# A two-block transformer on one core: shared up product in units 1 and 2, two slab rooms outside the ring, late constants, head sums spread over gate tiles

## The chip, the cores and the metric

One Trainium2 chip; the program runs on one core. The metric is device time in microseconds of the whole program (one launch), the median of three runs. Engines: TensorE (PE) multiplies, VectorE (DVE), ScalarE (ACT) and GpSimd (POOL) work on vectors, and SyncE (SP) issues most of the weight transfers.

## The reference, cut to what matters

Sequence of T = 256 tokens, width D = 1024, batch 1, everything in float32.

```python
# block 1
h = rms_norm(x, g1) * (1 + scale1) + shift1              # six modulation vectors = silu(c) @ w_ada + b
na_q, na_k, na_v, q_lat, kv_lat, k_rot, gate_na, gate_mla = split(h @ w_in)
y_na  = neighbourhood_attention(8 heads of 64)
qm, km = latent attention: 8 heads of 96, each head's row RMS-normed over its 96 values
x += gate1 * ((sigmoid(gate_na) * (y_na @ w_proj_na) + sigmoid(gate_mla) * (y_mla @ w_proj_mla)) @ w_out)
h2 = rms_norm(x, g2) * (1 + scale2) + shift2
# 64 experts, 8 per token (4 of 8 groups first), each 1024 -> 256 -> 1024
routed = sum over chosen experts of gate * (silu(h2 @ w_eg) * (h2 @ w_eu)) @ w_ed
shared = (silu(h2 @ w_sg) * (h2 @ w_su)) @ w_sd
x += gate2 * (routed + shared)
# block 2, for x and for a context ctx of 256 rows (the context does not depend on x)
layer 0: gMLP gating beside Fourier mixing, on x and on ctx
layer 1: windowed attention of x over x and ctx, 16 heads
out = rms_norm(x, final_g)
```

## The kernel before, in words

Each engine's program is written out by hand, one `block` function per engine, with semaphores between them. There is no planner at run time; the order of each engine's instructions is the order in the code.

**Weights as slabs.** All large weights are cut into slabs of 1 MiB (128 partitions x 2048 floats). They go through a ring of 11 slots (`ring`, `RING = 11`). PE's code asks for slabs in its own order (`ask`, `take_slab`) and says by `ends` which of its steps gives a slot back. SP's function (L1388) loads the slabs in the order asked, each once the slot's former slab has ended (`load`, `given_back`). From the first expert on, slots are handed out in the order in which they are given back, not round the ring. One slab has a room of its own: `first_slab` in the arena.

**Block 1.** PE computes the projections from `hT` (the normed input, features on partitions), slab by slab. `gate_tiles(s)`, s = 0 to 7, makes the 16 sigmoid gates, two tiles of 8 products each per slab (each float32 product stands as two records in the trace). Between slabs 4 and 5 stand the head sums of the latent attention: for each of four groups of two heads, the sums of squares of the queries (8 records of one column, L831) and of the keys (one product of 512 columns, L838). ACT squares a group into `sqt` (queries in half 0, keys in half 1), PE sums it, and ACT may write the half again once it is read. ACT takes roots, and DVE reciprocals (L2088). Then come both attentions (`early_attention`), the projections (L857), `w_out` (L873), and the router (`router`, L883).

**Routing.** From the router's result DVE makes scores, group choice, top 8, and the order of experts by how many tokens each has (`ordered`). Slots of tokens per expert, and the gates (`gates_made`), follow. PE has as filler four modulation slabs (`LAST_FILL`), then the shared gate product (`shared("shg", ...)`) and the shared up product (`shared("shu", ...)`, both L922), before it turns the gates by expert and gathers token rows for the first units (`gather`, L982).

**Expert stage.** 24 units; a unit of kind P holds two experts, X two of unequal slots, Q four with 32 slots each. Unit 0 takes the two experts fixed in advance (their slabs are loaded before the ranking is known: six slabs, `first_ones`); all other experts' addresses wait for `ordered`. Per unit: first half of the gate and up product (one slab per expert, L1140), the gate column, second half (one slab each), gathers for a later unit, `scatter` of the unit before into four banks (L1004), turns, and the down product (one slab each, L1183). After each half stand the steps of the table `CONTEXT`: the row `2: z0 z1 fa0 | fb0 fa1` puts z0, z1 and fa0 after the first half of unit 2 and fb0 and fa1 after its second half. They are block 2's layer 0 for the context: z and v tiles (16 and 4, one slab per two tiles, L1095 and L1101), Fourier steps fa and fb, sp, o tiles (L1039), the sum of squares and norm, and `shd`, the shared down product. DVE and ACT follow in `context_out`.

**Constants.** POOL loads `cs2` (Fourier tables, rotary tables, window mask, spatial bias; 1408 KB, L1511) and `spat` after the residual of block 1. ACT loads the router weights after the fourth pair of the early attention.

After the experts come the context keys (L1258), layer 0 and layer 1 of block 2 for x, and the output.

Of the kernel before, what the change touches and what calls it, by code (L numbers as in the profile page):

```python
# [19 lines left out]
ALU = mybir.AluOpType  # L20
# [74 lines left out]
15: | o1 o2  # L95
16: o3 |
18: o4 | o5
19: o6 |
20: | o7
21: squares0 | sum0  # L100
# [36 lines left out]
C2_AT, C2_W = offsets(C2_WIDTHS)  # L137
V_AT, V_W = offsets(V_WIDTHS)
# [3 lines left out]
def build(nc, x_d, ctx_d, consts_d, consts2_d, vecs_d, pos_d, rpb_d, spat_d, router_d, slabs_d, exp_d, out_d):  # L142
    with ExitStack() as ctx:
# [39 lines left out]
        def cc(name, a=0, b=None):  # L183
            src, at = (cs, C_AT) if name in C_AT else (cs2, C2_AT)
            lo, hi = at[name]
            return src[:, lo + a:(hi if b is None else lo + b)]
# [101 lines left out]
        rows = ar(4096, KT * (T + 1), KT, T + 1)  # L288
# [8 lines left out]
        cs2 = ar(11008, C2_W + 512)  # L297
        spat_bias = cs2[:, C2_W:C2_W + 512]
        spat = ar(11008 + C2_W + 512, 512, 4, 128)
# [8 lines left out]
        with nc.sbuf_tensor("bias_room", [P, 8 * RUN + 1024], F32) as bias_room:  # L308
            braw = bias_room[:, 0:8 * RUN].rearrange("p (a b) -> p a b", a=8)
            bmask = bias_room[:, 8 * RUN:8 * RUN + 1024].rearrange("p (a b) -> p a b", a=2)  # L310
            wr = bias_room[:, 0:512].rearrange("p (a b) -> p a b", a=8)
# [133 lines left out]
        def _(pe):  # L445
# [379 lines left out]
            o = open_group("mq_sums", 3)  # L825
            for g in range(4):
                pe.wait_ge(S("sq_m"), 2 * g + 1)
                for h in range(2):
                    for t in range(TT):
                        c = 4 * g + 2 * h + t  # L830
                        mm = mmul(o[:, c:c + 1], sqt[0:96, 0, 256 * h + P * t:256 * h + P * t + P], ones[0:96, 0:1],  # L831
                                  start=True, stop=True)
# [4 lines left out]
                pe.wait_ge(S("sq_m"), 2 * g + 2)  # L837
                close_group(mmul(open_group(("msum", 4 + g), 1 + g % 2)[0:96, :], ones[0:96, 0:96], sqt[0:96, 1, :], start=True, stop=True), ("msum", 4 + g))  # L838
            for s in (5, 6, 7):
                gate_tiles(s)  # L840
# [44 lines left out]
            for k in range(KT - 1):  # L885
                router(k)
# [6 lines left out]
            close_group(router(KT - 1), "rtT")  # L893
# [115 lines left out]
            def expert_slabs(m, j):  # L1009
                if m == 0:  # L1010
                    if j == 0:
                        first_ones.extend(ask(("exp", r, i)) for i in range(3) for r in UNITS[0][1])
                        held["ahead"] = ask(("ab", 4))
                    got = [(arrived(n), n) for n in first_ones[2 * j:2 * j + 2]]
                else:
                    got = [take_slab(("exp", r, j)) for r in UNITS[m][1]]
                return [w.rearrange("p (k c) -> p k c", c=512) for w, _ in got], [n for _, n in got]
# [48 lines left out]
            def context_step(m, kind, i, b):  # L1066
# [10 lines left out]
                if kind in ("squares", "norm"):  # L1077
                    return
                if kind == "o":
# [3 lines left out]
                if kind == "z":  # L1083
                    if i == 0:
                        pe.wait_ge(S("first_in"), 16)
                    elif i == 4:
                        held[kind] = held["ahead"]
                        arrived(held[kind])
                    elif i % 2 == 0:
                        held[kind] = take_slab(("ab", 2 + i // 2))[1]  # L1090
                    w = first_slab if i < 2 else eight(held[kind])
# [11 lines left out]
                elif kind == "fa":  # L1103
                    if i == 0:
                        pe.wait_ge(S("const2_in"), 32)
# [10 lines left out]
                if kind in ("z", "v") and i % 2 and (kind, i) != ("z", 1):  # L1116
# [272 lines left out]
        def _(sp):  # L1389
            expert_of = {}  # L1390
# [16 lines left out]
            def load(n):  # L1407
# [1327 lines left out]
```

## Time and profile before

| | us |
|---|---|
| median of 3 runs | 1102.38 (1100.65 to 1103.85) |
| the profiled execution, own time | 1107.04 |
| its span | 1105.2 |
| PE busy | 1057.4 (96%) |
| DVE busy | 394.6 (36%) |
| ACT busy | 283.6 (26%) |
| mean DMA rate over the span | 303 GB/s (335.12 MB) |
| mean granted clock | 0.988 |

The span runs from the first to the last instruction. Busy time of PE counts pipelined matmuls whose ends are modelled, so a slow clock shows as busy, not idle. The DMA share is the mean busy share of the 16 DMA engines, and it can come out slightly above 1. A line number such as L1140 is that of the program of before.

### The profile page before, as it was taken

How to read it: one execution, taken by the hardware profiler on the slowest of the kernel's cores; microseconds unless marked ns; L12 is line 12 of the kernel's file. 1: busy time of each engine (PE TensorE's matmuls, PEld its weight loads, DVE VectorE, ACT ScalarE, POOL GpSimd, SP SyncE). 2: the span in 40 equal slices, each digit the busy share in tenths (PEclk: the TensorE clock that was granted, in tenths of full speed). 3: DMA queues.
4: the chain of work that ended last, by engine and by line, in shares of the span. 5: the costliest groups of instructions: out<-in, count | busy, mean ns of one | idle time of the engine just before them, and what ended most of it. 6: DMA issues, size and time to landing. Idle time of an engine off the chain costs nothing.

```text
span 1105.2 us, 15950 instructions
## 1 busy us (share of the span) xinstructions
PE 1057.4 (96%) x6296; PEld 730.0 (66%) x6296; DVE 394.6 (36%) x1034; ACT 283.6 (26%) x656; POOL 52.4 (5%) x85
## 2 busy tenths in 40 slices
PE   6999999999999999899989999999789999999998
PEld 4786776688755665465546565555358888887567
DVE  1398966523532223112212212121333021523941
ACT  3124134510431112112211111123222111213941
POOL 0000202013100000000000000001000001100001
PEclk9999989999999999999999999999999999999999
DMA  9999387964769999999999999999996334310000
GB/s 385 354 420 420 125 338 273 419 271 153 297 256 411 419 421 420 421 420 421 421 421 421 421 421 421 421 421 421 419 417 272 125 118 152 112 39 1 1 2 38
DMA packets 48555, 335.12 MB, mean 303 GB/s; under 512 B 5440, under 2 KB 6816, under 8 KB 8672
## 3 DMA queue, kind: packets, MB, share of 16 engines
q1 hardware_dynamic: 46080, 329.01, 73.2%
q10 hardware_dynamic: 2176, 3.37, 1.0%
q0 software_dynamic: 224, 1.70, 0.4%
q8 instruction: 51, 0.84, 0.3%
q14 instruction: 24, 0.20, 0.0%
HBM read 333.02 MB, written 1.05 MB: 302 GB/s over the span
## 4 chain that ended last, share of the span: by engine, by line
PE 81%; DMA 12%; DVE 4%; ACT 1%; issue 1%; SPq 1%; DVEq 0%; ACTq 0%
PE bank L1140 12%; PE bank L567 12%; DMA ring<-experts 11%; PE bank L1183 6%; PE bank L1282 5%; PE bank L1095 4%; PE bank L982 3%; PE bank L486 3%; PE bank L1370 3%; PE bank L857 3%; PE bank L1325 2%; PE bank L873 2%; PE bank L1004 2%; PE bank L697 2%; PE bank L633 2%; PE bank L1039 2%
## 5 line engine op out<-in xcount | busy, mean ns | idle before, releaser
L1140 PE MATMUL bank<-ring,arena 128*32 128x512 f32 (+1 forms) x1120 | 177.2, 608 | 17.4 <-DMA ring<-experts 16.4
L1140 PEld LDWEIGHTS bank<-ring,arena 128*32 128x32 f32 (+1 forms) x1120 | 54.0, 122 | 121.5 <-issue 120.4
L567 PE MATMUL bank<-hT,ring 128*128 128x256 f32 x576 | 128.4, 383 | 0.7 <-ACT hT L1564 0.7
L567 PEld LDWEIGHTS bank<-hT,ring 128*128 128x128 f32 x576 | 109.6, 192 | 21.5 <-issue 6.9
L1183 PE MATMUL bank<-ring,conds 128*32 128x512 f32 (+1 forms) x560 | 87.5, 595 | 4.3 <-DMA ring<-experts 2.6
L1725 ACT ACTIVATE arena<-bank,mod 128x256 f32<-128x256 f32 x96 | 40.2, 470 | 98.6 <-PE bank L982 98.5
L2384 DVE SCALAR_TENSOR_TENSOR conds<-bank,gcol,conds 128x256 f32<-128x256 f32 x24 | 11.6, 484 | 143.7 <-ACT conds L1756 125.8
L2399 DVE TENSOR_TENSOR yhalf<-bank,yhalf 128x512 fp32r<-128x512 f32 x48 | 33.2, 692 | 78.8 <-ACT yhalf L1764 78.8
L1501 POOL TENSOR_TENSOR hT<-hT 128x256 f32<-128x256 f32 x30 | 21.7, 723 | 822.1 <-ACT hT L1558 820.6
L982 PE MATMUL bank<-picked,halves 128*128 128x256 f32 x384 | 57.8, 293 | 0.7 <-ACT arena L1725 0.7
L1183 PEld LDWEIGHTS bank<-ring,conds 128*32 128x32 f32 (+1 forms) x560 | 27.4, 119 | 46.7 <-issue 39.2
L1282 PE MATMUL bank<-hT,ring 128*128 128x256 f32 x256 | 57.0, 379 | 0.0
L982 PEld LDWEIGHTS bank<-picked,halves 128*128 128x128 f32 x384 | 48.8, 188 | 10.7 <-issue 8.9
L2158 DVE SCALAR_TENSOR_TENSOR resid<-bank,mod,resid 128x256 f32<-128x256 f32 (+1 forms) x48 | 19.7, 437 | 93.6 <-PE bank L1370 25.8
L1282 PEld LDWEIGHTS bank<-hT,ring 128*128 128x128 f32 x256 | 48.3, 190 | 6.6 <-issue 0.2
L1095 PE MATMUL bank<-hT,ring 128*128 128x256 f32 x224 | 50.3, 382 | 0.1
L1004 PE MATMUL bank<-yhalf,selT 128*128 128x512 f32 x192 | 48.5, 394 | 0.0
L1095 PEld LDWEIGHTS bank<-hT,ring 128*128 128x128 f32 x224 | 42.1, 190 | 7.9 <-issue 2.1
L1756 ACT ACTIVATE conds<-bank 128x256 f32<-128x256 f32 x24 | 9.2, 383 | 145.3 <-PE bank L1140 145.3
L1764 ACT CAST yhalf<-bank 128x512 fp32r<-128x512 f32 x48 | 28.1, 585 | 59.1 <-PE bank L1183 59.1
L1984 DVE SCALAR_TENSOR_TENSOR arena<-ring,conds,arena 128x256 f32<-128x256 f32 x84 | 40.7, 485 | 3.0
L1004 PEld LDWEIGHTS bank<-yhalf,selT 128*128 128x128 f32 x192 | 34.4, 188 | 7.8 <-issue 1.6
(415 smaller groups left out, 1444.5 us busy)
## 6 DMA issues: line engine op xcount, KB each, us to landing
ring<-experts SPq DMA_DIRECT2D x188, 1024.0 KB, 14.5
ring<-stream SPq DMA_DIRECT2D x119, 1024.0 KB, 12.3
ring<-experts SPq DMA_DIRECT2D x8, 512.0 KB, 15.4
arena<-consts POOLq DMA_DIRECT2D x1, 1408.0 KB, 9.4
resid<-x SPq DMA_DIRECT2D x1, 1024.0 KB, 5.1
resid<-ctx ACTq DMA_DIRECT2D x1, 1024.0 KB, 9.9
arena<-stream SPq DMA_DIRECT2D x1, 1024.0 KB, 8.3
bias_room<-rpb ACTq DMA_DIRECT2D x2, 438.0 KB, 5.6
```

The source lines that it names most:

```text
L486: mm = mmul(o[32 * g:32 * g + 32, 0:256], (silc if which == "ada1" else silc2)[:, 4 * kk + g, at:at + 32], w[:, 4 * kk + g, :], start=firs ...
L567: mm = mmul(o[:, 0:n_tok], w[:, k, t * P:(t + 1) * P], hT[:, k, 0:n_tok], start=(k == 0), stop=(k == KT - 1))
L857: mm = mmul(o[:, 0:256], w[:, 512 * k + P * t:512 * k + P * t + P], yT[:, y0 + k, :], start=(k == 0), stop=(k == 3))
L982: mm = mmul(o[:, 256 * (d % 2):256 * (d % 2) + n], halves[:, q, t, P * d:P * d + P], picked[:, t, 0:n], start=(t == 0 and q == 0), stop=(t ...
L1004: mm = mmul(bank[b][:, :], selT[:, b // 2, :], yhalf[:, q, 512 * (b % 2):512 * (b % 2) + 512], start=m == 0 and q == 0, stop=last and q == 1)
L1095: mm = mmul(o[:, 0:T], w[:, k, P * (i % 2):P * (i % 2) + P], hT[:, k, T:2 * T], start=(k == 0), stop=(k == KT - 1))
L1140: mm = mmul(o[at:at + n_slots, :], xg_of(m, kk)[:, at:at + n_slots], w[g][:, k, :], start=(kk == 0), stop=(kk == KT - 1))
L1183: mm = mmul(o[at:at + n_slots, :], aT[:, f, at:at + n_slots], w[g][:, 2 * c + f, :], start=(f == 0), stop=(f == 1))
L1282: mm = mmul(o[:, 0:T], eight(n)[:, k, (i % 2) * P:(i % 2 + 1) * P], hT[:, k, 0:T], start=(k == 0), stop=(k == KT - 1))
L1725: last = a.activation(to[:, i, 0:n], bk(("xg", j, c))[:, 256 * i:256 * i + n], ACT.Identity, bias=mod1[:, 24 + 2 * c + i:25 + 2 * c + i])
L1984: last = v.scalar_tensor_tensor(out=at, in0=w[:, k, :], scalar=silc[:, k, 15:16], in1=at, op0=ALU.mult, op1=ALU.add)
L2399: last = v.tensor_tensor(yhalf[:, 1, 512 * c:512 * c + 512], bk(("y", m, c))[:, :], yhalf[:, 0, 512 * c:512 * c + 512].bitcast(F32), ALU.s ...
```

## The change

The table of context steps, with the shared up product (`shu`) in it and everything later moved:

```diff
-CONTEXT = """1: z4 z5 |
-2: z0 z1 fa0 | fb0 fa1
-3: fb1 z2 |
-4: z3 z6 z7 | fa2
-5: | fb2
-6: fa3 | fb3 v0
-8: v1 | v2 v3
-9: shd0 z8 | z9 z12
-11: z13 |
-12: sp0 sp1 z10 z11 z14 |
-13: | z15 sp2
-14: | sp3 fold0 o0
-15: | o1 o2
-16: o3 |
-18: o4 | o5
-19: o6 |
-20: | o7
-21: squares0 | sum0
+CONTEXT = """1: shu0 |
+2: | shu1 z4 z5
+3: z0 z1 | fa0
+4: fb0 | fa1
+5: fb1 z2 |
+6: | z3 z6 z7 fa2
+7: | fb2 fa3
+8: fb3 v0 | v1
+9: v2 | v3
+10: shd0 |
+12: z8 z9 | z12 z13 sp0 sp1
+13: | z10
+14: z11 z14 |
+15: z15 | sp2
+16: sp3 | fold0 o0
+17: o1 |
+18: o2 o3 | o4
+19: o5 o6 |
+20: o7 squares0 |
+21: sum0 |
 22: norm0 | norm1"""
```

PE no longer computes the up product before the gathers; its slab is asked for behind five slabs of unit 0 and kept until the second half of unit 2:

```diff
             shared("shg", 0, 0, range(6, KT))
-            shared("shg", 1, 7, range(0, 2))
             sort_by_rank("slots_by_rank", "slots_by_expert", 0, 5)
-            shared("shg", 1, 7, range(2, KT))
+            shared("shg", 1, 7, range(0, KT))
             ends(ng, ("shg", 1))
-            _, shared_slab["shu"] = take_slab(("shu", 0))
-            shared("shu", 1, 1, range(KT))
-            shared("shu", 0, 3, range(KT))
-            ends(shared_slab["shu"], ("shu", 0))
```

DVE's part of it (`by_token`, `shared_hidden`) moves to the same two context steps. Two slabs get rooms outside the ring: the first expert slab of unit 0 goes to `keys_room` (the later keys and values), the slab of z4 and z5 to the first half of `hT`:

```diff
+            idle_slab = hT[:, :, 0:T]
...
-                        first_ones.extend(ask(("exp", r, i)) for i in range(3) for r in UNITS[0][1])
-                        held["ahead"] = ask(("ab", 4))
-                    got = [(arrived(n), n) for n in first_ones[2 * j:2 * j + 2]]
+                        first_ones.extend(ask(("exp", r, i)) for i in range(3) for r in UNITS[0][1][i == 0:])
+                        held["shu"] = ask(("shu", 0))
+                        pe.wait_ge(S("early_in"), 16)
+                        got = [(keys_room[:, :], None), (arrived(first_ones[0]), first_ones[0])]
+                    else:
+                        got = [(arrived(n), n) for n in first_ones[2 * j - 1:2 * j + 1]]
...
                     if not expert_of:
+                        full(sp, "sum2")
+                        sp.dma_start(idle_slab, slabs_d[slabs_at["ab"] + 4].rearrange("p (k c) -> p k c", k=8)).then_inc(S("idle_in"), 16)
                         sp.wait_ge(S("ordered"), 1)
...
+                if old is not None and slab_end[old] == ("pm", 7) and not early:
+                    early.append(n)
+                    done(sp, ("na", "s", 7))
+                    sp.dma_start(keys_room[:, :], exp_d[expert(UNITS[0][1][0]), 0]).then_inc(S("early_in"), 16)
```

The constants are split; rotary tables and mask (`cs_late`, 1536 columns of 128 x 4 bytes, 0.79 MB) come after the experts. The places of `cs2`, `spat_bias`, `spat`, `rows` and `wr` in the arena change to fit:

```diff
-            pool.dma_start(cs2, consts2_d).then_inc(S("const2_in"), 16)
+            pool.dma_start(cs2, consts2_d[:, 0:DFT_W]).then_inc(S("const2_in"), 16)
+            pool.dma_start(spat_bias, consts2_d[:, C2_W:C2_W + 512]).then_inc(S("const2_in"), 16)
             pool.dma_start(spat, spat_d).then_inc(S("const2_in"), 16)
             partial_sums("sq4c", side=1)
+            pool.wait_ge(S("sq3"), 1)
+            pool.dma_start(cs_late, consts2_d[:, DFT_W:C2_W]).then_inc(S("late_in"), 16)
```

The head sums are split into groups and placed among the gate tiles of slabs 5 and 6 (`key_sums(g)` one product of 512 columns, `query_sums(g)` the 8 records of one column, `gate_part` half a tile: 4 of its 8 products):

```diff
+            key_sums(0)
+            key_sums(1)
+            gate_slab[5] = take_slab(("in", 13))[1]
+            gate_part(5, 0, 1, range(0, 4))
+            key_sums(2)
+            key_sums(3)
+            gate_part(5, 0, 1, range(4, KT))
+            gate_part(5, 1, 2, range(0, 4))
+            query_sums(0)
+            gate_part(5, 1, 2, range(4, KT))
...
+            query_sums(1)
+            gate_slab[6] = take_slab(("in", 14))[1]
+            gate_part(6, 0, 0, range(0, 4))
+            query_sums(2)
+            gate_part(6, 0, 0, range(4, KT))
+            gate_part(6, 1, 7, range(0, 4))
+            query_sums(3)
+            gate_part(6, 1, 7, range(4, KT))
...
+            gate_tiles(7)
```

ACT squares keys 0 and 1, then takes gate slab 4, keys 2 and 3, queries 0 and 1, the root of the key sums, gate slab 5, queries 2 and 3, gate slab 6, the root of the query sums, gate slab 7. DVE's work on the query sums moves behind its four reciprocals.

The router's eighth product moves ahead of the row sums, and the transfer of its weights from the fourth to the seventh pair of the attention:

```diff
-            for k in range(KT - 1):
-                router(k)
+            for k in range(KT):
+                mm = router(k)
+            close_group(mm, "rtT")
             pe.wait_ge(S("sq2_part"), KT - 2)
...
-            close_group(router(KT - 1), "rtT")
```

## Rows read from the trace of the kernel before

**Rows 1.** Page, part 1: busy us (share of the span) and instructions of each engine.

```profile
PE 1057.4 (96%) x6296; PEld 730.0 (66%) x6296; DVE 394.6 (36%) x1034; ACT 283.6 (26%) x656; POOL 52.4 (5%) x85
```

**Rows 2.** Windows: length, busy of five engines, then clock, DMA share, GB/s.

```profile
293.00:299.00 6.00, 6.00 (x44) 4.82 (x37) 4.79 (x23) 5.56 (x10) 0.00 (x0) 1.00 0.89 367
...
314.00:321.00 7.00, 6.07 (x38) 2.91 (x38) 3.86 (x13) 3.67 (x7) 0.00 (x0) 1.00 0.11 44
...
345.00:430.00 85.00, 85.00 (x598) 49.85 (x596) 24.01 (x83) 16.14 (x37) 0.00 (x0) 1.00 1.01 420
430.00:795.00 365.00, 349.47 (x2114) 198.78 (x2110) 79.54 (x185) 73.20 (x159) 4.34 (x6) 1.00 1.01 421
...
843.00:850.00 7.00, 7.00 (x34) 6.15 (x34) 3.23 (x9) 1.04 (x4) 0.00 (x0) 1.00 0.49 180
```

**Rows 3.** Waits of PE, 345 to 830: us in total, times, longest.

```profile
PE bank L1140 <- DMA ring<-experts: 16.4, 11, 5.2
PE bank L1183 <- DMA ring<-experts: 2.6, 3, 1.7
```

**Rows 4.** Chain that ended last, 780 to 835: start us, us, what.

```profile
795.42 16.00 DMA ring<-experts
```

**Rows 5.** Windows, as in rows 2, of the head sums.

```profile
143.00:146.00 3.00, 3.00 (x13) 2.00 (x12) 0.76 (x2) 1.33 (x3) 0.00 (x0) 0.58 0.96 360
...
150.00:154.00 4.00, 4.00 (x9) 2.50 (x8) 1.39 (x6) 2.01 (x3) 0.00 (x0) 0.54 1.01 428
```

**Rows 6.** Chain that ended last, 136 to 180, as in rows 4.

```profile
140.62 0.79 PE bank L831 x8
141.40 0.94 PE bank L838 x2
142.34 0.89 PE bank L831 x8
...
144.85 1.50 PE bank L831 x8
...
151.57 8.02 PE bank L567 x32
159.59 0.56 PE bank L511 x4
160.15 7.10 PE bank L567 x32
...
174.91 1.00 PE bank L486 x16
```

**Rows 7.** Timeline of ACT: start us, us, engine, line, operation, out<-in.

```profile
141.50 0.63 ACT L1639 ACTIVATE arena<-arena 96x512 f32<-96x512 f32 x1 [0.46 <-PE bank L831]
```

**Rows 8.** Timeline of DVE, as in rows 7.

```profile
154.52 3.35 DVE L2088 RECIPROCAL pT<-pT 96x512 f32<-96x512 f32 x1 [1.41 <-ACT pT L1553]
```

**Rows 9.** Timeline of PE, from the shared products to unit 0's down product.

```profile
300.65 9.83 PE L922 MATMUL bank<-arena,ring 128*128 128x257 f32 x44
...
316.42 3.65 PE L1140 MATMUL bank<-ring,arena 128*64 128x512 f32 x16 [0.93 <-ACT arena L1725]
...
326.79 3.65 PE L1183 MATMUL bank<-ring,conds 128*64 128x512 f32 x16
```

**Rows 10.** Timeline of DVE: the gates are divided.

```profile
303.93 0.42 DVE L2279 TENSOR_SCALAR pr<-pr,pT 128x64 f32<-128x64 f32 x2
```

**Rows 11.** Timeline of SyncE: issues of expert slabs around unit 0.

```profile
299.29 11.71 SPq L1426 DMA_DIRECT2D ring<-experts  x4
...
310.66 0.34 SPq L1426 DMA_DIRECT2D ring<-experts  x1
...
320.25 0.85 SPq L1426 DMA_DIRECT2D ring<-experts  x2
```

**Rows 12.** Page, part 6: KB each, us from issue to landing.

```profile
arena<-consts POOLq DMA_DIRECT2D x1, 1408.0 KB, 9.4
```

**Rows 13.** Timeline of PE: three context tiles in a row, unit 4.

```profile
400.52 10.63 PE L1095 MATMUL bank<-hT,ring 128*128 128x256 f32 x48
```

More of the change, by code:

```diff
@@ L137 @@
 C2_AT, C2_W = offsets(C2_WIDTHS)
+DFT_W = C2_AT["cos2"][0]
 V_AT, V_W = offsets(V_WIDTHS)
@@ L824, in _, with key_sums, query_sums @@
                 gate_tiles(s)
-            o = open_group("mq_sums", 3)
-            for g in range(4):
-                pe.wait_ge(S("sq_m"), 2 * g + 1)
+            def key_sums(g):
+                pe.wait_ge(S("sq_m"), g + 1)
+                o = open_group(("msum", 4 + g), 4 + g % 2)
+                close_group(mmul(o[0:96, :], ones[0:96, 0:96], sqt[0:96, g % 2, :], start=True, stop=True), ("msum", 4 + g))
+            def query_sums(g):
+                pe.wait_ge(S("sq_m"), 5 + g)
+                o = open_group("mq_sums", 3) if g == 0 else bk("mq_sums")
                 for h in range(2):
@@ L836, in _, with gate_part @@
                     close_group(mm, "mq_sums")
[L837 to L840, printed above, removed]
+            def gate_part(s, t, b, ks):
+                n = gate_slab[s]
+                o = open_group((f"gt{s}", t), b) if ks[0] == 0 else bk((f"gt{s}", t))
+                for k in ks:
+                    mm = mmul(o[:, 0:256], eight(n)[:, k, t * P:(t + 1) * P], hT[:, k, 0:256], start=(k == 0), stop=(k == KT - 1))
+                if ks[-1] == KT - 1:
+                    close_group(mm, (f"gt{s}", t))
+            gate_slab = {}
+            key_sums(0)
[8 more added lines that the diff above has]
+            gate_part(5, 1, 2, range(4, KT))
+            ends(gate_slab[5], ("gt5", 1))
+            for i in SIDE_SUMS[5]:
+                side_sum(i)
+            query_sums(1)
[6 more added lines that the diff above has]
+            gate_part(6, 1, 7, range(4, KT))
+            ends(gate_slab[6], ("gt6", 1))
+            for i in SIDE_SUMS[6]:
+                side_sum(i)
+            gate_tiles(7)
             pe.wait_ge(S("qk_ready"), 8)
@@ L1078, in context_step @@
                     return
+                if kind == "shu":
+                    if i == 0:
+                        shared_slab["shu"] = held["shu"]
+                        arrived(held["shu"])
+                    shared("shu", i, b, range(KT))
+                    if i == 1:
+                        ends(shared_slab["shu"], ("shu", 1))
+                    return
                 if kind == "o":
@@ L1115, in context_step @@
                 close_group(mm, (kind + "c", i))
-                if kind in ("z", "v") and i % 2 and (kind, i) != ("z", 1):
+                if kind in ("z", "v") and i % 2 and (kind, i) not in (("z", 1), ("z", 5)):
                     ends(held[kind], (kind + "c", i))
@@ L1628, in _, with squares_of @@
                 gate_tiles(s)
-            for gg in range(4):
-                for kind, src in ((0, qm), (1, km)):
-                    if gg == 1 and kind == 0:
-                        gate_tiles(4)
-                    act.wait_ge(S("m_in"), 4 * kind + gg + 1)
-                    if gg and kind == 0:
-                        act.wait_ge(S("mq_read"), gg)
-                    elif gg:
-                        full(act, ("msum", 3 + gg))
-                    a.activation(sqt[0:96, kind, :], src[0:96, 2 * gg:2 * gg + 2, :].rearrange("p a b -> p (a b)"), ACT.Square).then_inc(S("sq_m"), 1)
+            def squares_of(src, gg):
+                v = src[0:96, 2 * gg:2 * gg + 2, :].rearrange("p a b -> p (a b)")
+                a.activation(sqt[0:96, gg % 2, :], v, ACT.Square).then_inc(S("sq_m"), 1)
+            for gg in (0, 1):
+                act.wait_ge(S("m_in"), 4 + gg + 1)
+                squares_of(km, gg)
+            gate_tiles(4)
+            for gg in (2, 3):
+                act.wait_ge(S("m_in"), 4 + gg + 1)
+                full(act, ("msum", 2 + gg))
+                squares_of(km, gg)
+            for gg in (0, 1):
+                full(act, ("msum", 6 + gg))
+                squares_of(qm, gg)
+            root(1, pT[:, :, :].rearrange("p a b -> p (a b)"), "mk", 2048, 96)
+            gate_tiles(5)
+            for gg in (2, 3):
+                act.wait_ge(S("mq_read"), gg - 1)
+                squares_of(qm, gg)
+            gate_tiles(6)
             full(act, "mq_sums")
@@ L2323, in fold_tokens, with shared_hidden @@
                 v.tensor_tensor(to[:, P + 1:2 * P], src[:, 1:P], back, ALU.subtract).then_inc(S(tag), 1)
+            def shared_hidden():
+                dve.wait_ge(S("shg_made"), 2)
+                for t in range(2):
+                    done(dve, ("shu", t))
+                    v.scalar_tensor_tensor(out=shu[:, t, :], in0=shu[:, t, :], scalar=shifted[:, 2 + t:3 + t], in1=shg[:, t, :],
+                                           op0=ALU.add, op1=ALU.mult).then_inc(S("sh_act"), 1)
             def context_out(kind, i):
```

62 lines of the change are left out of this document (31 added, 31 removed).

## The prediction

> **What bounds the kernel now.** I read the page first: TensorE (PE) is busy 96% of 1105.2 us [rows 1], so there is little idle time to win by itself; what matters is where PE's work is slow and where the end is set by something else. The table of stretches shows DMA engines that are full from 345 to 795 us, 421 GB/s at a share of 1.01 [rows 2]: the expert stage streams weights without a break. The waits of PE say the same from the other side: 16.4 us for expert slabs in the gate and up products, and the chain that ended last runs over a 16.00 us piece of expert DMA right up to 811.42, where the last down product starts [rows 3, 4]. So the stage ends when its stream ends. At 421 GB/s a slab of 1 MiB (1.0486 MB) takes 2.49 us, and PE's pace in the stage costs nothing as long as it gives slots back in time. The end moves only if the stream starts earlier, has fewer bytes, or has fewer holes. Ahead of about 299 us nothing on the path waits for DMA; there the chain is PE, instruction by instruction. In it one stretch is odd: the head sums at 143 to 154 us run at a granted clock of 0.58 to 0.54 [rows 5].
>
> **Head sums spread over gate tiles.** The chain of that stretch [rows 6]: a query group (8 matmuls of one column) takes 0.79 us at full clock and 1.50 at half, a key group (2 of 512) 0.94; the gate tiles behind them take 8.02 instead of 7.10. From 140.62 to the first scores at 175.91 PE needs 35.3 us. The work afterwards is the same: four key groups, 4 x 0.94 = 3.8; four query groups, 4 x 0.84 = 3.4 (mean of the 0.79 and 0.89 at full clock); three gate slabs, 3 x 7.10 = 21.3; two side sums, 2 x 0.56 = 1.1; the mod1 slab 1.0. Sum 30.5, that is 4.8 less, if the clock stays full. Are the new waits covered? The squares of keys 0 and 1 need no sums and stand ahead of gate slab 4 on ACT; keys 2 and 3 and queries 0 and 1 each wait for one group of sums and have at least half a gate tile (1.78 us) against a 0.63 us square [rows 7]. Queries 2 and 3 stand behind the square root, a change of tables and gate slab 5 on ACT; that lies beside 7.1 us of gate slab 5 on PE. VectorE's four reciprocals of 3.35 us [rows 8] follow the root, which comes some 4 us sooner, and have the gate tiles beside them; its rq operations, now behind them, have some 3 us. I take -4.8. Bounds: 0 (the clock falls anyway) to -5.0. PE then runs 4.8 us ahead to the router; the slabs there are not late, since PE has no DMA wait in it.
>
> The Trainium skill ("TensorE: Matmul & The Clock Gate", the section on a second HAM failure mode, psum-queue depth-cycling) says that an engine that idles briefly between groups of matmuls, again and again, can make the clock swing between its two levels. PE shows no idle time in 140 to 154 us and the clock falls all the same, so the trace neither proves nor excludes it; by that rule eight hand-overs among gate tiles could bring the fall back, which is my first rival.
>
> **Router order.** The eighth router product now stands ahead of the row sums, which close about 0.5 us later; the row scale and what follows on VectorE (rtS copy, scores, mask, order) come 0.4 us later. PE has filler there, so I charge 0.4 to the routing chain (bounds 0 and 0.6). The router weights are fetched some 15 us later, still 60 us ahead of use: 0.
>
> **Shared up product out of the prelude.** The 44 records from 300.65 hold 12 of the gate product and 32 of the up product: at 0.22 us each the up product is 7.1 us [rows 9]. Taken out, PE reaches the turn of the gates at 303.3; but VectorE finishes the gates only at 304.35 [rows 10], 1.1 us later, and with the 0.4 above at 304.75. So gathers and unit 0 come 7.1 - 1.5 = 5.6 us sooner: from 316.42 to 310.8 in the old time (all times here leave out the 4.8, which moves everything alike). The two halves come back as 3.55 us each in units 1 and 2, where the stream sets the end: 0, as long as slots are free in time.
>
> **Slab rooms and slots, which set the stream.** Expert loads of unit 1 need the ranking, at 299.29. SyncE then issues four slabs only, from 299.29 to 310.66, the last two on slots that the shared products give back, and nothing until unit 0's first half returns slots at 320.25 [rows 11]. Four slabs are 10.0 us of transfer in 20.96: 11.0 us dry; the window 314 to 321 at a share of 0.11 shows it [rows 2]. Another 0.3 is lost before unit 0's down product ends. Afterwards: one expert slab lies in the room of the later keys and one context slab in hT, so with the up slab kept in the ring four slots are free at the ranking instead of two, and the gate slab's slot makes five (free at 303.3). The bytes still to come are the same on both sides (186 expert slabs and 13 others), so only the holes count. From 299.7: five slabs last to 312.15, the first slot of unit 0 comes back at 310.8 + 3.65 = 314.45: 2.3 dry. One slab, to 316.95, then two slots at 318.0: 1.1 dry. Two slabs, to 323.0, then two slots at 310.8 + 14.0 = 324.8 (unit 0 took 316.42 to 330.4): 1.8 dry. Behind them unit 1 gives four slots 3.6 us later, and two slabs cover 5.0. Dry time 5.2, and 0.4 for the later ranking: 5.6 against 11.3. Gain 5.7. Bounds: 0, if the freed time is lost again to a full ring, to -9, if unit 0 started at once and all but the first hole closed.
>
> Can PE use it? It starts 5.6 sooner, has 7.1 more to do, and has 19 us of DMA waits in the stage [rows 3]; it would still wait about 12 us, so the stream remains the bound.
>
> **Late constants.** Of 1408 KB [rows 12] 0.79 MB (1.9 us) move behind the experts. Where they were, the stretch 293 to 299 is not full, at a share of 0.89 [rows 2], so all that was asked for was over before the ranking's loads: 0 on the path. Where they go, DMA drops to a share of 0.49 at 843 to 850 [rows 2] and PE waits for no slab after the experts: 0. Without that cover it would cost 1.9.
>
> **Sum.** -4.8 - 5.7 = -10.5 us. The profiled execution took 1107.04 us with a span of 1105.2; it would take 1096.5. It is 4.7 us above the median of the timed runs, 1102.38, at which the same sum gives **1091.9 us**.
>
> **Rivals.** (1) The clock falls in the spread sums too. For: a query group is one column wide and the clock fell in the midst of such groups [rows 5, 6]. Against: each now has 1.8 us of dense gate work on both sides, and the gate tiles behind ran at their full-clock 7.10 again. The first term is lost: 1102.4 - 5.7 = 1096.7. (2) The ring is full more often than I count, and the stream's gain goes: 1102.4 - 4.8 = 1097.6. For: steps moved behind second halves put off the release of slots. Against: DMA stayed at 1.01 over 345 to 430, with a run of 10.63 us of context tiles in it [rows 2, 13]. (3) Slower: the same mechanism at its worst, in units 2 and 6. In unit 2, after the second half, stand 10.65 us of tiles, then 4.6 of gathers, scatter and turns and 3.6 of down product: 18.9 us in which three slots (7.5 us) come back, so 11.4 dry if no other is free; in unit 6 19.9 us against six slots (14.9), 5.0 dry. Together 16.4: 1091.9 + 16.4 = 1108.3. It decides from 13.8 us dry on; the same row of 10.63 us speaks against it, and the ring starts with two slots more.
>
> **How the numbers follow.** Forecast 0.64, rival 1 0.17, rival 2 0.11, both at once (about no change) 0.04, rival 3 0.04. A measurement here tells 0.3% (3.3 us) from no change. Faster by more: the first three, less a little for a partial loss of both: 0.89; within it 0.07; slower 0.04. The range, 1088.5 to 1098.5, holds the forecast with its bounds and rivals 1 and 2; below, it takes in that more of the holes closes.
>
> **What would show it.** Right: granted clock 1.00 from 140 to 171, the first scores near 171; the ranking's first load near 295 with four slabs in a row; unit 0 at 306; no window under a share of 0.9 after 325; the last expert wait over near 801, and PE waiting about 12 us for experts. Wrong: half-clock rows in the gate tiles (rival 1); a share under 1.0 in units 2 to 7 (rivals 2, 3); or PE without any wait for experts at the end, which would say that PE has become the bound.

## The result, and the profile after

The changed kernel took 1099.6 us (median of 20 runs; one execution of 2777.72 us stands alone and is left out of what follows, the others lie between 1093.77 and 1102.18). The kernel before took 1103.66 us beside it (median of 20, 1100.2 to 1108.65). The ratio is 0.9948, interval [0.9931, 0.9965]: 5.7 us faster, where 10.5 were forecast, and the time is above the upper end of the range by 1.1 us. The two medians by themselves lie 4.1 us apart. Here and below, a gain in us that stands beside a ratio is the ratio's unless medians are named; the two can differ by a microsecond or more, as the runs of one kernel spread over 2 to 9 us. The profiled execution took 1099.61 us, its span is 1097.8, 7.4 less than that of before. The first row of the page, busy time by engine, answers to [rows 1]:

```profile
PE 1055.3 (96%) x6296; PEld 726.0 (66%) x6296; DVE 394.4 (36%) x1034; ACT 286.6 (26%) x658; POOL 54.0 (5%) x87
```

PE is 2.1 us less busy with the same 6296 matmuls. The windows (length; busy of PE, PEld, DVE, ACT, POOL; clock; DMA share; GB/s) answer to [rows 2, 5]:

```profile
143.00:146.00 3.00, 3.00 (x12) 1.98 (x11) 0.93 (x3) 0.87 (x3) 0.00 (x0) 1.00 0.93 380
176.00:178.00 2.00, 2.00 (x16) 0.73 (x17) 1.80 (x10) 1.22 (x5) 1.50 (x3) 0.51 0.73 307
286.00:288.00 2.00, 2.00 (x10) 1.80 (x9) 1.35 (x12) 1.31 (x3) 0.00 (x0) 0.50 1.00 414
314.00:321.00 7.00, 6.56 (x38) 3.44 (x36) 1.57 (x4) 2.06 (x5) 0.00 (x0) 1.00 0.90 327
345.00:430.00 85.00, 84.41 (x606) 49.53 (x606) 22.93 (x76) 15.59 (x35) 0.00 (x0) 1.00 1.01 420
430.00:795.00 365.00, 352.56 (x2104) 201.69 (x2100) 76.51 (x180) 71.73 (x156) 4.34 (x6) 0.99 1.01 420
803.00:806.00 3.00, 1.74 (x12) 0.52 (x16) 0.00 (x0) 0.00 (x0) 0.00 (x0) 0.68 1.04 427
```

Two of the forecast's steps are in the first and the fourth row: the head sums now run at a clock of 1.00, and the hole at 314 to 321 us is closed (share 0.90, from 0.11). What was not forecast is in the second, third and last: the clock is down to half at 176 us, where attention starts, at 286 us, in the routing, and again at the last expert wait. The chain that ended last, from the head sums to the first scores and the first slabs behind them (start us, us, what), answers to [rows 6]; L855 is the gate tiles, L836 the key sums, L844 the query sums, L574 a gate slab by itself, L610 the scores, L493 slabs of modulation:

```profile
134.49 7.10 PE bank L574 x32
141.59 1.72 PE bank L836 x4
143.31 1.73 PE bank L855 x8
...
150.22 0.79 PE bank L844 x8
151.00 1.83 PE bank L855 x8
...
163.74 7.10 PE bank L574 x32
170.84 1.00 PE bank L493 x16
171.84 1.07 PE bank L610 x7
...
175.23 0.10 DVE mod L1983
175.33 0.04 issue
175.38 1.47 PE bank L610 x6
176.85 4.88 PE bank L493 x64
```

A query group takes 0.79 us, a gate half tile 1.8, the gate slab 7.10: all at full clock. Then PE waits for the modulation vector that DVE ends at 175.33, and the 64 matmuls behind it take 4.88 us; at full clock they take 3.66 (a row below). At the end of the stream the same view, of after and then of before, shows the last down product:

```profile
792.08 11.94 DMA ring<-experts
804.02 0.24 issue
804.26 5.22 PE bank L1232 x32
```

```profile
811.42 0.24 issue
811.66 3.64 PE bank L1183 x32
```

The last wait ends 7.4 us sooner, and 1.6 of that are given back in one product. PE's waits of 345 to 830 us (total, times, longest), which answer to [rows 3], fall from 19.0 to 14.1 us, near the 12 forecast:

```profile
PE bank L1189 <- DMA ring<-experts: 10.7, 4, 5.2
PE bank L1232 <- DMA ring<-experts: 3.4, 1, 3.4
```

SyncE issues five slabs in a row behind the ranking (four from 298.49 to 302.19, the fifth at 302.88), as predicted, where four were spread over 11 us before [rows 11]. Then it still waits for a slot, until unit 0's first half gives some back at 312.71:

```profile
298.49 3.70 SPq L1477 DMA_DIRECT2D ring<-experts  x4
312.71 4.37 SPq L1477 DMA_DIRECT2D ring<-experts  x3
```

So smaller holes are left, as the forecast had them: the DMA share is 0.78 at 313 to 316 us and 0.57 at 322 to 325.

Where the 7.4 us of span come from, stretch by stretch, each from PE's timelines of the two profiles:

| stretch | before, us | after, us | difference |
|---|---|---|---|
| start to the end of gate slab 4 | 140.45 | 141.43 | +1.0 |
| to the first scores | 35.4 | 30.3 | -5.1 |
| first scores to the second score group | 8.2 | 9.9 | +1.7 |
| second group to the router's start | 98.56 | 98.56 | 0 |
| router to the shared products | 10.7 | 12.3 | +1.5 |
| shared products to unit 0 | 23.1 | 16.4 | -6.7 |
| unit 0 to the end of the last wait | 495.2 | 495.4 | +0.1 |
| last down product | 3.6 | 5.2 | +1.6 |
| the rest | 289.9 | 288.3 | -1.6 |

(The two cuts of the third and fourth line: 184.00 and 282.56 us before, 181.66 and 280.22 after.) The first and the last line are no effect of the change that these profiles show: up to 141 us PE does the same in both, and the fall of the clock at 16 to 24 us lies a little differently. The last line is one more fall, at 1057 to 1062 us behind a pause of 1.69 us. All 14 profiles have that pause and only this one of before has the fall; without it the first product takes 2.28 us and the second 1.95, 1.6 us less in all:

```profile
1056.98 3.14 PE L619 MATMUL bank<-cs,arena 128*128 128x128 f32 x16 [1.69 <-DVE arena L2033]
1060.05 2.71 PE L633 MATMUL bank<-pr,keys_room 128*64 128x256 f32 x16
```

### The profile page after: what moved, and what is told of

Its sections match the earlier page's. It is cut to its first block, busy times and chain, and to the rows that moved or that the text cites. A ratio compares the mean times of both kernels' runs of the same rounds, so it can differ in the third digit from the quotient of the medians.

```text
span 1097.8 us, 15950 instructions
## 1 busy us (share of the span) xinstructions
PE 1055.3 (96%) x6296; PEld 726.0 (66%) x6296; DVE 394.4 (36%) x1034; ACT 286.6 (26%) x658; POOL 54.0 (5%) x87
## 4 chain that ended last, share of the span: by engine, by line
PE 90%; DMA 4%; DVE 4%; ACT 1%; issue 1%; SPq 0%; DVEq 0%; ACTq 0%
PE bank L1189 14%; PE bank L574 10%; PE bank L1232 7%; PE bank L1144 5%; PE bank L1331 5%; PE bank L1021 4%; DMA ring<-experts 4%; PE bank L1043 3%; PE bank L493 3%; PE bank L1081 3%; PE bank L1419 3%; PE bank L901 3%; PE bank L1374 3%; PE bank L917 3%; PE bank L704 2%; PE bank L640 2%
## 5 line engine op out<-in xcount | busy, mean ns | idle before, releaser
L1189 PE MATMUL bank<-ring,arena 128*32 128x512 f32 (+1 forms) x1112 | 176.9, 605 | 11.3 <-DMA ring<-experts 10.7
L574 PE MATMUL bank<-hT,ring 128*128 128x256 f32 x512 | 113.0, 381 | 0.7 <-ACT hT L1622 0.7
L574 PEld LDWEIGHTS bank<-hT,ring 128*128 128x128 f32 x512 | 96.5, 190 | 18.1 <-issue 5.4
L1331 PE MATMUL bank<-hT,ring 128*128 128x256 f32 x256 | 57.0, 379 | 0.0
L1331 PEld LDWEIGHTS bank<-hT,ring 128*128 128x128 f32 x256 | 48.3, 190 | 6.6 <-issue 0.2
L1144 PE MATMUL bank<-hT,ring 128*128 128x256 f32 x192 | 43.2, 382 | 0.0
L1616 ACT ACTIVATE hT<-resid 128x256 f32<-128x256 f32 x48 | 17.9, 413 | 89.6 <-DVE resid L2225 89.6
L1144 PEld LDWEIGHTS bank<-hT,ring 128*128 128x128 f32 x192 | 36.0, 190 | 7.2 <-issue 2.5
```

The costliest lines, as they stand in the source:

```text
L574: mm = mmul(o[:, 0:n_tok], w[:, k, t * P:(t + 1) * P], hT[:, k, 0:n_tok], start=(k == 0), stop=(k == KT - 1))
L1144: mm = mmul(o[:, 0:T], w[:, k, P * (i % 2):P * (i % 2) + P], hT[:, k, T:2 * T], start=(k == 0), stop=(k == KT - 1))
L1189: mm = mmul(o[at:at + n_slots, :], xg_of(m, kk)[:, at:at + n_slots], w[g][:, k, :], start=(kk == 0), stop=(kk == KT - 1))
L1331: mm = mmul(o[:, 0:T], eight(n)[:, k, (i % 2) * P:(i % 2 + 1) * P], hT[:, k, 0:T], start=(k == 0), stop=(k == KT - 1))
```

## The experiments

"Before" is 1105.65 us on the chip of the first four, 1104.82 us for the next four and 1106.47 us for the last two timed ones; what counts is the ratio.

**e1: the spread head sums alone**, in the kernel before.

```diff
+            key_sums(0)
+            key_sums(1)
+            gate_slab[5] = take_slab(("in", 13))[1]
+            gate_part(5, 0, 1, range(0, 4))
+            key_sums(2)
...
+            gate_tiles(7)
```

> The kernel before with the spread head sums as the only edit. Theory G (given back): the stretch from the end of gate slab 4 to the first scores is 5 us shorter at a granted clock of 1.00, but the clock falls right behind it, where the attention starts (176 to 180 us), and perhaps at the router, and gives back 1.5 to 3.5 us; time -1.5 to -3.5 us. Rival H (the head sums keep their gain, what is missing was lost in the rest of the change): -4.5 to -5 us.

1103.85 us, ratio 0.9975 [0.9963, 0.9986]: 2.8 us, not 4.8 (the medians differ by 1.8). Its profile keeps the head sums at full clock, 5.1 us below those of before, and PE's timeline (start us, us, line, operation, [idle before <- releaser]) shows where part of that goes:

```profile
174.64 2.07 PE L603 MATMUL bank<-arena 64*128 64x256 f32 x6 [1.29 <-DVE mod L1962]
176.64 4.34 PE L486 MATMUL bank<-ring,conds 128*32 128x256 f32 x64
```

The six score matmuls behind the 1.29 us pause take 2.07 us; in the profiles without the fall they take 1.13. From the first scores to the second score group this profile needs 1.7 us more than before, and from unit 0 to the last down product another 1.7 (496.95 against 495.2).

**e2: everything but the head sums**, which stand as before.

```diff
-            key_sums(0)
...
+            o = open_group("mq_sums", 3)
+            for g in range(4):
+                pe.wait_ge(S("sq_m"), 2 * g + 1)
```

> The changed kernel with the head sums put back as before. Theory G: the rest is worth what the ledger of the two traces shows, unit 0 some 6.7 us sooner and the stream's last wait as much, less what the clock takes at the router (1.5): -4 to -6 us. Rival H: -1 to -2 us.

1100.51 us, ratio 0.9943 [0.9924, 0.9962]: 6.3 us, against the 5.7 forecast for this half. The two halves alone are worth 2.8 and 6.3 us, together 9.1; the whole change gave 5.7, and 7.4 in e10. Whether the halves add is not settled: the intervals are 1.5 to 4.1 us for e1, 4.2 to 8.4 for e2, 3.9 to 7.6 for the change and 5.0 to 9.8 for e10. The fall at attention is in e1 already, so it is not something that the halves do to each other.

**e3: the eighth router product behind the row sums again**, all else changed. With the new order DVE ends 0.52 us too late for the turned logits (L949), with the old one PE has no pause there, but reaches them no sooner, as it does other work in that time: they start 3.95 us behind the router's start with the new order (e10, no fall) and 4.09 with the old one (before).

```diff
-            for k in range(KT):
-                mm = router(k)
-            close_group(mm, "rtT")
+            for k in range(KT - 1):
+                router(k)
...
+            close_group(router(KT - 1), "rtT")
```

> The changed kernel with the eighth router product behind the row sums again. Theory R: the pause of 0.52 us before the turned logits (284.17 in the changed kernel), which the new order makes, is what lets the clock fall at 285 to 289; without it the clock stays at 1.00 there and the time is 1 to 2 us under the changed kernel's (ratio to before about 0.9935). Rival P (the fall comes with one-column and short products, whatever the order): fall still there, same time as the changed kernel.

1097.24 us, ratio 0.9917 [0.99, 0.9933]. PE's timeline in the routing, of the changed kernel and then of e3:

```profile
284.17 0.66 PE L949 MATMUL bank<-cs,pr 128*128 128x64 f32 x4 [0.52 <-DVE pr L2240]
...
285.49 1.06 PE L545 MATMUL bank<-hT,ones 128*128 128x256 f32 x2
286.34 2.62 PE L942 MATMUL bank<-cs,arena 128*128 128x128 f32 x12
```

```profile
281.65 0.66 PE L949 MATMUL bank<-cs,pr 128*128 128x64 f32 x4
...
282.86 0.59 PE L545 MATMUL bank<-hT,ones 128*128 128x256 f32 x2
283.29 1.47 PE L942 MATMUL bank<-cs,arena 128*128 128x128 f32 x12
```

The same 14 matmuls take 3.68 us behind the pause and 2.06 without it. In this profile the fall at the start of attention is absent too, though its pause is there (1.28 us); of the six profiles with the spread sums and this pause it is the only one without the fall. Nothing in e3's edit touches that place, so part of its gain over the changed kernel, 2 to 3 us by the ratios, can be chance: its six runs have mean clocks of 0.991 to 0.994, those of e10 0.988 to 0.991.

**e4: two slabs of modulation ahead of the scores that wait for the modulation vector**, all else changed. PE has this work anyway, four slabs of it, right behind those scores.

```diff
                 scores(0)
+                for f in FIRST_FILL[:2]:
+                    ada_slab(*f)
                 ada_fold(1)
                 scores(1)
-                for f in FIRST_FILL:
+                for f in FIRST_FILL[2:]:
                     ada_slab(*f)
```

> The changed kernel with two modulation slabs put between the first scores and the fold of the quarters, so that PE does not stand 1.28 us for the modulation vector. If that pause brings the fall at 176 to 180 us, the clock is 1.00 there, and the time is 1.7 (half-clock stretch) to 3 us (with the pause) under the changed kernel's. If the fall comes from the 64-row and 32-column products around it, it stays, and only up to 1.3 us goes.

1094.6 us, ratio 0.99 [0.9882, 0.9917]: 11.05 us faster than before. PE's timeline of e4, and then two rows of e3, which has the pause but not the fall:

```profile
171.67 1.93 PE L493 MATMUL bank<-ring,conds 128*32 128x256 f32 x32
173.53 0.63 PE L525 MATMUL bank<-cs,quarters 128*128 128x32 f32 x4
174.09 1.48 PE L610 MATMUL bank<-arena 64*128 64x256 f32 x8
175.50 1.93 PE L493 MATMUL bank<-ring,conds 128*32 128x256 f32 x32
```

```profile
174.36 1.13 PE L610 MATMUL bank<-arena 64*128 64x256 f32 x6 [1.28 <-DVE mod L1983]
175.41 3.66 PE L493 MATMUL bank<-ring,conds 128*32 128x256 f32 x64
```

The pause of 1.28 us is gone with its fall. From the first scores to the router's start e4, e5 and e9 need 105.9 us each, e3 with the pause and no fall 106.8, and e1, the changed kernel and e10, with pause and fall, 108.4, 108.5 and 110.0. So the filled pause is worth 0.9 us by itself and the fall 1.6 to 3.1.

**e5: both**, e3's and e4's edits together.

```diff
                 scores(0)
+                for f in FIRST_FILL[:2]:
+                    ada_slab(*f)
...
+            close_group(router(KT - 1), "rtT")
```

> The changed kernel with both edits together: two modulation slabs before the fold of the quarters, and the eighth router product behind the row sums. If the two places are what the change gave back, the gains add up: ratio to before 0.987 to 0.989 (some -12 to -14 us), no half-clock stretch between 140 and 420 us. If each edit had only lucky runs, the ratio stays at 0.990 or above.

1095.47 us, ratio 0.9917 [0.989, 0.9943]. The clock falls only at 16 to 24, at 544 and at 800 us in its profile. I had expected the two gains to add, to 0.987 to 0.989. They don't, and it is no faster than e4: with the attention pause out, the router order is worth nothing that these runs can show (e4's own profile has the 0.52 us pause at the turned logits and no fall behind it).

**e6: the late constants alone**, in the kernel before.

```diff
-            pool.dma_start(cs2, consts2_d).then_inc(S("const2_in"), 16)
+            pool.dma_start(cs2[:, 0:DFT_W], consts2_d[:, 0:DFT_W]).then_inc(S("const2_in"), 16)
...
+            pool.wait_ge(S("sq3"), 1)
+            pool.dma_start(cs2[:, DFT_W:C2_W], consts2_d[:, DFT_W:C2_W]).then_inc(S("late_in"), 16)
```

> The kernel before with only the late constants (rotary tables and mask fetched after the sums of squares behind the experts). The prediction's step: 0, ratio 1.000 within its interval. Rival: the 1408 KB held up the first slabs or the context slab ahead of the ranking, and without them something on the path comes sooner: -1 to -2 us.

1105.25 us, ratio 1.0005 [0.9986, 1.0024]: nothing that the runs show, as predicted; the interval still allows 1.5 us of gain. Its profile told more than its time. It has the old head sums, and the clock did not fall in them. The chain there (L832 query sums, L839 key sums, L568 gate slab):

```profile
140.27 0.79 PE bank L832 x8
141.06 0.94 PE bank L839 x2
...
145.76 0.80 PE bank L832 x8
146.56 1.08 PE bank L839 x2
147.64 6.91 PE bank L568 x32
...
170.87 1.07 PE bank L604 x7
```

From 140.11 to the scores it needs 30.7 us, with the old order. The forecast had priced the spread sums at 30.5 and measured 30.3: the new order saves 0.4 us in an execution whose clock stays up (one profile shows this). What it is worth beyond that is the fall that it takes away.

**e7: the first expert slab back in the ring**, its room of the later keys unused, all else changed.

```diff
-                        first_ones.extend(ask(("exp", r, i)) for i in range(3) for r in UNITS[0][1][i == 0:])
+                        first_ones.extend(ask(("exp", r, i)) for i in range(3) for r in UNITS[0][1])
...
-                    sp.dma_start(keys_room[:, :], exp_d[expert(UNITS[0][1][0]), 0]).then_inc(S("early_in"), 16)
```

> The changed kernel with the first expert slab of unit 0 in the ring again: one slot fewer when the ranking is known. By the slot count (a stream that is dry until unit 0 gives slots back) the last expert wait comes one slab, 2.5 us, later against the ranking, time +2 to +2.5 us over the changed kernel. Rival (PE, not the stream, sets the end of the stage): 0 to +0.5.

1099.33 us, ratio 0.9954 [0.9932, 0.9976], as the changed kernel. From the ranking's first load to the end of the last wait it needs 505.9 us (296.17 to 802.07), the changed kernel 505.8 (298.49 to 804.26). I had expected 2.5 more. The reason I give is argued and not shown: a slab in that room holds no slot, but it gives none back either when unit 0's first half ends, and that is where the stream was dry. The same stretch is 505.6 to 507.7 us in the six profiles with both rooms, so that a worth of 1 or 2 us would not be seen in one profile.

**e8: both rooms back**, e7 and the context slab asked into the ring as well.

```diff
+                        held["ahead"] = ask(("ab", 4))
...
-                        sp.dma_start(idle_slab, slabs_d[slabs_at["ab"] + 4].rearrange("p (k c) -> p k c", k=8)).then_inc(S("idle_in"), 16)
```

> The changed kernel with both slabs in the ring again: two slots fewer. By the slot count +5 us over the changed kernel, that is about the time of before: the early unit 0 alone is then worth next to nothing. Rival (PE sets the end): 0 to +1.

1101.41 us, ratio 0.9967 [0.995, 0.9985]. Ranking to last wait is 509.7 us (296.30 to 806.00), 3.9 more than with the rooms and 2.7 less than the 512.4 of before (512.2 and 512.3 in e12 and e11). I had expected 5 us more, about the time of before; the time is 1.4 us above e7 and 2.1 above the changed kernel by the ratios. So of the 6.6 us that the stream gained, 2 to 4 are the room in hT, nothing that can be seen is the room of the keys, and the 2.7 that are left go with everything else that moved, the earlier unit 0 above all.

**e9: e5 without the keys' room.**

```diff
-                        got = [(keys_room[:, :], None), (arrived(first_ones[0]), first_ones[0])]
...
+                    got = [(arrived(n), n) for n in first_ones[2 * j:2 * j + 2]]
```

> The changed kernel with both pauses out (two modulation slabs before the fold, router order back) and without the keys room (all six slabs of unit 0 in the ring). The last study showed the keys room worth nothing: its slab returns no slot when unit 0's first half ends, so what the stream gains ahead of unit 0 it lacks behind it. Expected: the same time as with the keys room, ratio to before 0.988 to 0.992. If the room has a worth that the noise hid, 2.5 us more: 0.993 to 0.994.

1095.48 us, ratio 0.99 [0.9877, 0.9922], as e4 and e5: the room is worth nothing here either.

**e10: the changed kernel again**, on the chip of e9.

> The changed kernel itself, beside the kernel before on the same chip. If the two parts add up (the head sums alone gave 0.9975, the rest alone 0.9943), 0.992; if the changed kernel has falls of the clock that neither part has by itself, 0.994 to 0.996, with a half-clock stretch at 172 to 180 us or 284 to 290 us in its profile.

1099.55 us, ratio 0.9933 [0.9911, 0.9955]: between the two values expected. Beside e9 (0.99) on the same chip it is some 4 us slower. Its profile has the fall at the start of attention again, longer:

```profile
174.54 2.07 PE L610 MATMUL bank<-arena 64*128 64x256 f32 x6 [1.29 <-DVE mod L1983]
176.54 5.85 PE L493 MATMUL bank<-ring,conds 128*32 128x256 f32 x64
```

**e11 and e12: the kernel before, one profiled run each**, to see how often the clock falls in its head sums.

> The kernel before, one more profile. Theory: the fall of the clock at the head sums comes in some executions only. In those with it the stretch from the end of gate slab 4 to the first scores takes 35 us and the profiled time is 1105 to 1108 us; without it 30.7 us and 1100 to 1103. Rival: the fall is there in every execution of this kernel, and the one profile without it (the kernel with late constants) owed that to its edit.

> The same as the run before it, for the count: each further execution either has the fall at 143 to 154 us (35 us for the stretch) or not (30.7 us). The prediction took it to be in all of them.

1105.95 and 1106.14 us. Both fall at 143 to 154 us and not at the start of attention (six score matmuls in 1.13 us behind a pause of 1.18 to 1.19 us). What all profiles say of the three places together:

| place | kernels | falls |
|---|---|---|
| head sums, old order | before, e2, e6, e11, e12 | 4 of 5 (not e6) |
| head sums, spread | after, e1, e3, e4, e5, e7 to e10 | 0 of 9 |
| start of attention, old sums, pause there | before, e2, e6, e11, e12 | 0 of 5 |
| start of attention, spread sums, pause there | after, e1, e3, e7, e8, e10 | 5 of 6 (not e3) |
| start of attention, spread sums, pause filled | e4, e5, e9 | 0 of 3 |
| routing, new router order | after, e2, e4, e7, e8, e10 | 2 of 6 (after, e2) |
| routing, old router order | before, e1, e3, e5, e6, e9, e11, e12 | 0 of 8 |

In the first five lines the counts differ clearly. Two of six against none of eight, in the last two, is too little to say that the router order matters. The profiles show falls in the expert stage too, behind PE's waits for an expert slab: behind all 21 waits of 3.4 to 6.2 us, behind 8 of 16 of 2.2 to 3.3 us, and behind none of 1.1 to 2.2.

## Why the prediction was wrong

The direction was right, and so was what the forecast said of the stream. The step that failed is its first term, the head sums: "I take -4.8", with "if the clock stays full" as its condition. It took the fall of the clock for a fixed cost of that stretch, and the rest of the kernel to be free of falls; measured alone the term is -2.8. That is 2.0 of the 4.8 us between 10.5 and 5.7. The times don't split the rest, which is within the intervals of e1, e2 and the change; in the profile it is the falls at the router and at the last down product.

- **Head sums, -4.8 forecast, -2.8 alone.** In its own stretch the term came out: 35.4 to 30.3 us, clock 1.00. But the fall was priced from one execution, and it is not in every one (e6 has 30.7 us with the old order), and with the sums spread one comes 30 us later, at the 1.28 us pause for the modulation vector, where the kernel before has a pause of 1.18 us and no fall. That gave 1.7 us back between the two score groups (8.2 to 9.9). The forecast weighed its condition, a full clock, for the spread sums only, and not for the next pause behind them. An estimate from the counts above: 5.1 us, gained in four executions of five, less 1.7 us, lost in five of six, is 2.7, close to the 2.8 measured.
- **Router order, 0.4 charged, bounds 0 and 0.6.** As a delay it was nothing: from the router's start to the ranking's first load before needs 16.7 us, and e4, e7 and e10, with the new order and no fall, 16.6. But the clock fell behind the new pause in two profiles of six, and in the ledger of the changed kernel that cost 1.5 us. Whether the new order brings this fall is not shown (0 of 8 with the old one; e5 is no faster than e4). The bounds left out that a pause can be followed by a fall, whose cost [rows 5, 6] show.
- **Last down product, not forecast.** 5.2 to 6.5 us behind the last expert wait in all eight profiles of kernels that have the spread sums together with the shared products in units 1 and 2, 3.64 us in the six of kernels that lack the one or the other. It cost 1.6 us in this profile. The fall itself is not new. Before, it lies one product earlier, under the last gate and up product of 32 records, behind the longest wait of the stage, and there it costs nothing, since PE then waits for the next slab anyway. In the changed kernel the longest wait at the end of the stage is that for the last slab of all. PE's timeline of before, and then of the changed kernel:

```profile
802.20 5.33 PE L1140 MATMUL bank<-ring,arena 128*32 128x512 f32 x32 [5.24 <-DMA ring<-experts]
811.66 3.64 PE L1183 MATMUL bank<-ring,conds 128*32 128x512 f32 x32 [1.75 <-DMA ring<-experts]
```

```profile
794.83 3.64 PE L1189 MATMUL bank<-ring,arena 128*32 128x512 f32 x32 [1.19 <-DMA ring<-experts]
804.26 5.22 PE L1232 MATMUL bank<-ring,conds 128*32 128x512 f32 x32 [3.43 <-DMA ring<-experts]
```

e11, e12, e1 and e6 have the slow product in the place of before (5.4 to 6.4 us, behind waits of 5.2 to 6.2). Only e2 has none at either place, and its longest wait there, 3.02 us, is the shortest of all. Why the longest wait moved from one slab to the next, and what would help against it, no run here was made to show.

- **Stream, -5.7 forecast, -6.3 alone, -6.6 in the profile.** Right in size. (The -5.7 had the 0.4 of the router in it, e2's -6.3 has all that the rest of the change does, and the -6.6 leaves out the 1.5 at the router; with it, -5.1.) The five slabs in a row, the closed hole at 314 us and the share of 1.01 from 345 us on came as forecast. Ranking to unit 0 was a little better, since the two shared products now behind the sort left no wait for the gates (they end at 302.66, PE comes at 302.72). Of its two rooms only one showed a worth (e7, e8).
- **Late constants and products moved to units 1 and 2, 0.** Right (e6; unit 0 to the last wait 495.2 and 495.4).

**The rivals.** Rival 1 was wrong as put: in nine profiles the spread sums never fell. Its kind of loss came at other places, and its time, 1096.7, is nearer the result than the forecast. The rule of the Trainium skill that stood beside it ("TensorE: Matmul & The Clock Gate", the section on a second HAM failure mode) speaks of brief idle stretches between groups; here single pauses of 1.28 and 0.52 us went with falls in five of six and two of six profiles, and the head sums fell without any idle time that the profile shows, so the measurements are on its side only in part. Rivals 2 and 3 were wrong: the share over 345 to 430 and over 430 to 795 us is 1.01 as before, and PE's waits for slabs went down and not up.

The ledger of what was lost between 10.5 and the 7.4 of the profile: 1.7 at attention, 1.5 at the router, 1.6 at the last product, 1.0 at the start, less 0.3 and 0.9 that the head sums and the stream gave above their terms, and less 1.6 in the tail: 3.0 in all, of 3.1. The 1.6 in the tail is the fall at 1057 us that only this profile of before has. The timed runs show 5.7 and not 7.4, as the profiled execution of before, 1107.04 us at a mean clock of 0.988, lies near the top of its runs (1100.2 to 1108.65), 3.4 us above their median. The forecast had noted such a distance, and carried the term to the median in full all the same. Its base was low too: 1102.38 is the median of three runs, 1103.66 that of twenty, which by itself moves the forecast to 1093.2.

**A version that is better than both** is e4: 1094.6 us, 0.99 [0.9882, 0.9917], 3.6 to 5.3 us below the changed kernel by the ratios. e5 and e9 can't be told from it. Its ratio is that of the forecast (1091.9 at 1102.38, 0.9905), but that is partly luck: 0.9 us of it is the filled pause itself, which the forecast did not have, and the slow last down product is still in it.

## What to carry to other kernels

A stretch at half clock in one profile is not a price: profile the kernel a few times and count in how many executions it is there before its gain is written into a sum. When a fall of the clock is taken out, look for the next pause of PE behind it, even one of little over 1 us behind which nothing fell before, and fill it with work that stands right behind it. A fall costs nothing where PE will wait for the next transfer anyway; so look at which product stands behind the last long wait of a stream. For a streamed ring, a room outside the ring is worth what it adds at the moment when the stream is dry: a slab whose slot would have come back just then gains nothing (argued from e7, not shown by itself).

## What the runs showed of the hardware

- The granted clock falls to 0.50, the lower of its two levels (1.2 of 2.4 GHz), at 146 to 150 us of before, with means of 0.58 and 0.54 in the windows around it, in a stretch in which PE has no idle time that the profile shows (busy ends are modelled), and it does so in four of five profiles of the same instructions there.
- Which pause is followed by a fall goes with what stood before it: the pause at the start of attention went with no fall in five profiles with the old head sums (1.18 to 1.19 us; four of them with a fall 25 us earlier, one with none) and with a fall in five of six with the spread ones (1.28 to 1.29 us). Whether it is the earlier fall itself, the new mix of work or the 0.1 us that decides is open; e6, with neither fall, speaks against the first, as one profile can.
- Long waits are followed by a fall each time: PE's 21 waits of 3.4 to 6.2 us for an expert slab, in 14 profiles, all had a product of 32 records behind them that took 4.9 to 6.6 us in place of 3.64; of the 16 waits of 2.2 to 3.3 us 8 had.
- The time of an execution goes with its mean clock. Of 57 timed executions of the kernel before, 21 at 0.987 to 0.988 took 1106.6 to 1108.4 us, 19 at 0.990 to 0.991 took 1104.7 to 1107.4, 11 at 0.992 to 0.994 took 1102.6 to 1104.2, and 6 at 0.995 to 0.997 took 1100.1 to 1101.2. So the spread of this kernel goes with how long the clock is down in an execution.
- One core's stream of 1 MiB slabs held 420 GB/s, at a share of 1.01, over the 450 us from 345 to 795.
